# A seven-product scheme for half of a feed-forward matrix, interleaved with tiles of the other matrix

## What is computed

```
f = rms_norm(h, g_ffn_pre)                       # 256 x 2048
f = square(relu(f @ w_ff1)) @ w_ff2              # w_ff1: 2048 x 8192, w_ff2: 8192 x 2048
h = h + rms_norm(f, g_ffn_post)
```

## Time and profile before

| | us |
|---|---|
| median of 3 runs | 2151.79 |
| lowest, highest | 2151.78, 2152.73 |
| profiled execution, first to last instruction (span) | 2150.6 |

### The profile page before, as it was taken

One profiled execution on the slowest core, in us unless ns is written; L12 is line 12 of the kernel. 1 busy time (PEld: TensorE's weight loads), 2 busy tenths in 40 slices (PEclk: granted clock), 3 DMA queues, 4 the chain that ended last, 5 costly groups with the idle time before them and its releaser, 6 DMA issues. The chain is left out here.

```text
span 2150.6 us, 29240 instructions
## 1 busy us (share of the span) xinstructions
PE 2125.1 (99%) x11602; PEld 1841.8 (86%) x11602; DVE 1361.9 (63%) x1979; ACT 1106.1 (51%) x1541; POOL 156.2 (7%) x78
## 2 busy tenths in 40 slices
PE   8999999999999999999999999999999999999998
PEld 7888888888988888888888888888888888888886
DVE  5554568875577558876578678766555555555555
ACT  4444554454464555555455455656435534544543
POOL 0000000000000000000007873000000000000000
PEclk9999999999999999999999999999999999999999
DMA  8666545655576655655656654646666666666664
GB/s 278 196 189 187 165 138 174 179 172 186 185 214 186 178 148 159 174 167 176 191 180 198 193 178 151 215 136 206 193 193 190 189 193 193 189 194 190 192 190 145
DMA packets 325031, 395.17 MB, mean 184 GB/s; under 512 B 20848, under 2 KB 252912, under 8 KB 324128
## 3 DMA queue, kind: packets, MB, share of 16 engines
q1 hardware_dynamic: 323104, 383.21, 59.0%
q0 software_dynamic: 1792, 10.10, 1.2%
HBM read 391.16 MB, written 2.10 MB: 183 GB/s over the span
## 5 line engine op out<-in xcount | busy, mean ns | idle before, releaser
L490 DVE TENSOR_TENSOR low<-raw,high 128x1024 fp32r<-128x1024 f32 (+2 forms) x672 | 809.9, 1209 | 639.0 <-ACT high L934 635.3
L934 ACT ACTIVATE high<-raw 128x1024 fp32r<-128x1024 f32 (+2 forms) x732 | 763.0, 1046 | 775.8 <-PE acc L682 201.7
L682 PE MATMUL acc<-xhl,high 128*128 128x512 f32 x3198 | 766.4, 391 | 0.0
L682 PEld LDWEIGHTS acc<-xhl,high 128*128 128x128 f32 x3198 | 587.0, 188 | 113.8 <-issue 0.7
L699 PE MATMUL acc<-xhl,low 128*128 128x256 f32 x3200 | 436.9, 286 | 1.9 <-DVE xhl L1792 1.4
L699 PEld LDWEIGHTS acc<-xhl,low 128*128 128x128 f32 x3200 | 414.4, 191 | 18.1 <-DVE xhl L1792 1.8
L686 PE MATMUL acc<-high,yhl 128*128 128x512 f32 (+1 forms) x1036 | 380.1, 373 | 2.2 <-DVE work L1718 1.6
L687 PE MATMUL acc<-high,yhl 128*128 128x512 f32 (+1 forms) x1036 | 378.8, 372 | 0.0
L702 PE MATMUL acc<-low,yhl 128*128 128x512 f32 (+1 forms) x1036 | 241.9, 374 | 0.2
L686 PEld LDWEIGHTS acc<-high,yhl 128*128 128x128 f32 x1036 | 195.2, 188 | 36.8 <-DVE work L1718 2.0
L687 PEld LDWEIGHTS acc<-high,yhl 128*128 128x128 f32 x1036 | 195.2, 188 | 33.8
(11 more groups left out here) (228 smaller groups left out, 1286.9 us busy)
## 6 DMA issues: line engine op xcount, KB each, us to landing
raw<-in_w_in SPq DMA_DIRECT2D x328, 512.0 KB, 3.7
raw<-in_w_ff SPq DMA_DIRECT2D x256, 512.0 KB, 3.9
raw<-in_w_out SPq DMA_DIRECT2D x91, 512.0 KB, 4.3
raw<-in_w_mem_kv SPq DMA_DIRECT2D x32, 512.0 KB, 5.0
raw<-in_w_in SPq DMA_DIRECT2D x16, 256.0 KB, 2.7
raw<-in_w_out SPq DMA_DIRECT2D x10, 256.0 KB, 2.8
x_nat<-in_mem SPq DMA_DIRECT2D x4, 512.0 KB, 7.8
x_nat<-in_x POOLq DMA_DIRECT2D x4, 512.0 KB, 6.4
```

Source lines behind the costliest of these rows:

```text
L490: eng.tensor_tensor(part(low, g), part(raw, g), part(high, g).bitcast(F32), ALU.subtract).then_inc(ready, 1)
L682: ins = pe.matmul(acc[:, 2 * (c.acc % 2) + s, :], wh[:, t, at], vhl, start=first, stop=last)
L934: act.activation(part(high, g), part(raw, g), ACT.Copy).then_inc(high_ready, 1)
```

## The change

The second matrix is cut into two column halves. In columns 0 to 1023, of the first 7168 hidden features, each group of 256 features is multiplied as a 2x2 by 2x2 product of blocks (128x128 by 128x512) by Strassen's scheme with seven products in place of eight; there are 28 such groups, four to a run. Their seven sums of the weight blocks are made by VectorE (`group_sums`), split by ScalarE (`split_h`) and VectorE (`split_l`), and the matching sums of the hidden features by GpSimd (`pair_sums`, four additions of 128x128 per pair of tiles). The seven products of a run stay in seven PSUM banks; after the run VectorE adds them to sums in SBUF (`sums_out`), and at the end mixes these into the result (`mix_sums`). Columns 1024 to 2047, and the last 1024 features of all columns, are plain "pieces" of one block each.

The first matrix, after its first 512 columns, comes in tiles of 128 columns and two blocks each (rows of 512 bytes in HBM), all accumulated in one PSUM bank (`feature_tile`), which ScalarE copies out (`tile_copy`) before the next tile. Between them stand the groups, cut in a high and a low half. The order is written out by hand in `ff_order`, and matching orders in the queues. The low part of a block is now written over the block itself, so its load waits until TensorE has used the block four back. The squares of x stand in ScalarE's queue ahead of the first period. The clearing of the sums in SBUF moves from VectorE to GpSimd.

The diff, cut to what the text speaks of (in the order of the file; `ff_period` and `piece_run` appear twice, first ScalarE's, then VectorE's):

```diff
-            add(("f2", q, n), a["w_ff2_2"][0], col, width=width, row0=D * q)
+    w = a["w_ff1_2"][0]
+    run(*[chunk(("f1", 0, j), w, 256 * j, width=256, flipped=True) for j in range(2)])
+    w2 = a["w_ff2_2"][0]
+    for kind, *at in FF_ORDER:
+        if kind == "tile":
+            add(("g1", at[0]), w, P * at[0], width=P, nk=8)
+        elif kind == "piece":
+            e, n, i = at
+            if i == 0:
+                chunk(("f2", e, n), w2, CW * n, row0=8 * P * e, kts=8)
+            place(by["f2", e, n], i)
...
+FF0 = BLOCK2 + BLOCK2_SLOTS
+TILES, TILES_AHEAD = 64, 4
+GROUPS, RUNS = 28, 7
+BESIDE = {0: (6, 7), 1: (None, 8), 2: (9, 10), 3: (None, 11)} | {j: (2 * j + 4, 2 * j + 5) for j in range(4, GROUPS)}
+def ff_order():
+    yield from (("tile", 4), ("tile", 5))
+    for j in range(GROUPS):
+        yield ("high", j)
+        if BESIDE[j][0] is not None:
+            yield ("tile", BESIDE[j][0])
+        yield ("low", j)
+        yield ("tile", BESIDE[j][1])
+        if j % 4 == 3:
+            yield from (("piece", j // 4, n, i) for n in (2, 3) for i in range(4))
+    for i in range(2):
+        for n in range(2):
+            yield ("piece", RUNS, n, i)
+            yield ("tile", 60 + 2 * i + n)
+    yield from (("piece", RUNS, n, i) for i in (2, 3) for n in range(2))
+    yield from (("piece", RUNS, n, i) for n in (2, 3) for i in range(4))
+FF_ORDER = list(ff_order())
+FF1 = FF0 + 8
+BLOCKS = FF1 + sum({"tile": 2, "piece": 1}.get(k[0], 0) for k in FF_ORDER)
+PRODUCTS = ((5, 1, 4), (6, 4, 5), (2, 2, 2), (3, 3, 7), (7, 5, 6), (4, 6, 3), (1, 0, 0))
+OUTS = (2, 3, 1, 5, 6, 7, 4)
...
         def low_part(eng, g, ready):
             eng.wait_ge(high_ready, g + 1)
-            eng.tensor_tensor(part(low, g), part(raw, g), part(high, g).bitcast(F32), ALU.subtract).then_inc(ready, 1)
+            out = part(rawr if g >= FF1 else low, g)
+            eng.tensor_tensor(out, part(raw, g), part(high, g).bitcast(F32), ALU.subtract).then_inc(ready, 1)
...
+            def feature_tile(n):
+                if n > TILES_AHEAD + 1:
+                    pe.wait_ge(tile_out, n - TILES_AHEAD)
+                    if n - 12 in range(0, 56, 8):
+                        pe.wait_ge(piece_out, 4 * ((n - 12) // 8) + 3)
+                bank = tile_bank(n)
+                for i, g in enumerate(by["g1", n].blocks):
+                    wh, wl = part(high, g), part(rawr, g)
...
+                    if i:
+                        with_low()
+                        ins = with_high()
+                    else:
+                        with_high()
+                        ins = with_low()
+                    ins.then_inc(block_used, 1)
...
+            def group_high(j):
+                pe.wait_ge(pair_ready, j + 1)
+                pe.wait_ge(split_high, 3 * j + 3)
+                for p, unit, n in PRODUCTS:
+                    if j % 4 == 0:
+                        product_released(j // 4, p)
+                    for hl in range(2):
+                        pe.matmul(bank_of[p], rows_of(hl, j, n), bset_r[:, j % 2, 7 + unit, :], start=j % 4 == 0 and hl == 0,
+                                  stop=False)
+            def group_low(j):
+                pe.wait_ge(split_low, 3 * j + 3)
+                for p, unit, n in PRODUCTS:
+                    ins = pe.matmul(bank_of[p], rows_of(0, j, n), bset_r[:, j % 2, unit, :], start=False, stop=j % 4 == 3)
+                ins.then_inc(group_used, 1)
...
+            def piece(e, n, i, rows=(0, 1)):
+                g, pair = by["f2", e, n].blocks[i], 4 * e + i
+                wh, wl = part(high, g), part(rawr, g)
+                banks = last_banks[n]
+                pe.wait_ge(pair_ready, pair + 1)
...
+            def x_squares(c):
+                act.wait_ge(norm_ready, norms(2, 2 * c + 1))
+                squares(x[:, :, CW * c:CW * c + CW], c, junk=ff_junk)
...
+            def tile_copy(n):
+                act.wait_ge(block_used, last_of(("g1", n)))
+                if n >= TILES_AHEAD + 2:
+                    act.wait_ge(pair_sq, n // 2)
+                act.activation(tcopy[:, n % 2, :], tile_bank(n), ACT.Copy).then_inc(tile_out, 1)
...
+            def ff_period(j):
+                n, b = next_blocks(j), BESIDE[j][0] is not None
+                p = {0: 2, 1: 3, 2: None, 3: 4}[j] if j < 4 else j + 1 if j % 4 else None
+                if j == 3:
+                    relu_of(p)
+                if j < 4 or j % 4:
+                    tile_copy(BESIDE[j - 1][1] if j else 5)
+                if b:
+                    round_block(n[2])
+                if j + 1 < GROUPS:
+                    split_h(j + 1, 0)
+                if p is not None and j != 3:
+                    relu_of(p)
+                if b:
+                    round_block(n[3])
+                if j + 1 < GROUPS:
+                    split_h(j + 1, 1)
+                    split_h(j + 1, 2)
+                if b:
+                    tile_copy(BESIDE[j][0])
+                if p is not None:
+                    pair_h(p)
+                m = n[4:6] if b else n[2:4]
+                round_block(m[0])
+                round_block(m[1])
+                return m[1] + 1
...
+            cross_out(("f1", 0, 0))
+            round_block(FF1 + 2)
+            relu_of(0)
+            round_block(FF1 + 3)
+            cross_out(("f1", 0, 1))
+            split_h(0, 0)
+            pair_h(0)
+            split_h(0, 1)
+            split_h(0, 2)
+            round_block(FF1 + 4)
+            tile_copy(4)
+            relu_of(1)
+            round_block(FF1 + 5)
+            pair_h(1)
+            for c in range(4):
+                x_squares(c)
+            for j in range(GROUPS):
+                g = ff_period(j)
+                if j % 4 == 3:
+                    piece_run(j // 4, g)
+            g = BLOCKS - 24
+            for b, task in enumerate((None, None, None, None, None, 60, None, None, 61, 30, None, None, 62, None, None, 63)):
+                if b >= 2:
+                    round_block(g + b)
+                if task in (60, 61, 62, 63):
+                    tile_copy(task)
+                if task == 63:
+                    relu_of(31)
+                    pair_h(31)
+                if b == 9:
+                    relu_of(30)
+                if b == 10:
+                    pair_h(30)
+            for b in range(16, 24):
+                round_block(g + b)
+                if b in (18, 19):
+                    act.wait_ge(sum_ready, sums("f2", b - 18))
+                    squares(m_cols(b - 18), b - 18, junk=tail[:, 2, :])
+            act.wait_ge(sum_ready, sums("f2", 2))
+            squares(m_cols(2), 2, junk=tail[:, 2, :])
             for s in range(ST):
-                act.wait_ge(sum_ready, sums("f2", NQ - 1, NF - 1) + s)
-                squares(mixed_cols(FCOLS[NF - 1]), NF - 1, (s,))
-                act.wait_ge(var_ready, 7 + s)
+                act.wait_ge(sum_ready, sums("f2", 3) + s)
+                squares(m_cols(3), 3, (s,), junk=tail[:, 2, :])
+                act.wait_ge(var_ready, 6 + s)
                 act.activation(std[:, s:s + 1], var[:, s:s + 1], ACT.Sqrt).then_inc(std_ready, 1)
...
+            def group_sums(g):
+                units = bset[:, g % 2]
+                dve.wait_ge(group_landed[g % 2][0], 16 * (g // 2 + 1))
+                dve.tensor_tensor(units[:, 1, :], units[:, 1, :], units[:, 0, :], ALU.subtract).then_inc(sum_step, 1)
+                dve.wait_ge(group_landed[g % 2][1], 16 * (g // 2 + 1))
+                dve.wait_ge(sum_step, 3 * g + 1)
+                dve.tensor_tensor(units[:, 4, :], units[:, 3, :], units[:, 1, :], ALU.subtract).then_inc(sum_step, 1)
+                dve.wait_ge(sum_step, 3 * g + 2)
+                t2 = units[:, 4, :].unsqueeze(1).broadcast_to([P, 2, CW])
+                dve.tensor_tensor(units[:, 5:7, :], t2, units[:, 0:3:2, :], ALU.subtract).then_inc(sum_step, 1)
...
+            def ff_period(j):
+                n, b = next_blocks(j), BESIDE[j][0] is not None
+                p = {0: 2, 1: 3, 2: None, 3: 4}[j] if j < 4 else j + 1 if j % 4 else None
+                if j == 3:
+                    fold_pair(p)
+                if j + 1 < GROUPS:
+                    group_sums(j + 1)
+                if p is not None and j != 3:
+                    fold_pair(p)
+                if b:
+                    low_block(n[2])
+                if b:
+                    low_block(n[3])
+                if j + 1 < GROUPS:
+                    for part_no in range(3):
+                        split_l(j + 1, part_no)
+                if j % 4 == 3:
+                    sums_out(j // 4, OUTS[:3])
+                if p is not None:
+                    pair_l(p)
+                m = n[4:6] if b else n[2:4]
+                low_block(m[0])
+                low_block(m[1])
+                return m[1] + 1
...
+            def piece_run(e, g):
+                p = 4 * e + 5
+                sums_out(e, OUTS[3:5])
```

(83 more changed lines are left out.)

367 lines of the change are left out of this document (260 added, 107 removed).

## The result

The changed kernel takes **2204.95 us** (median of 4 runs, 2204.15 to 2207.38) against 2152.26 for the kernel before (4 runs, 2151.78 to 2153.29): ratio **1.0245**, 95% interval 1.023 to 1.0259. The forecast was slower, but 2165 with a range to 2182; it missed by 40 us and lies outside its range.

A forecast was written before the change was run, and what follows sets the result against it. TensorE alone was taken to set the time of the feed-forward part. -19.1 + 3.6 + 3.5 + 2.3 + 9.4 + 1.5 + 11.4 = +12.6, say +13, on a span of 2150.6 gave 2165 us, range 2150 to 2182.

The forecast's parts named there:

- -19.1: Second matrix's groups: 28 groups with three matmuls less each at 0.228 us, -19.1 us, all on the path.
- TensorE's gaps at the seams: Start and end of feed-forward: TensorE waits 2.3 before first group, 9.4 before tile 6, then 2.7, 3.9 and 4.8 us.
- Additions: GpSimd's four 128x128 additions per pair: 0.5 us each, holding VectorE back by about that, 8 us a run.
- rival 3: The port: GpSimd's additions and VectorE's operations alternate, delaying ReLU and rounds in each run's pieces; 2182 us, chance 0.12.
- DMA: Steady state: tile blocks in 512-byte rows, 2.5 us per block, 13.3 of 15.9 us a period; fits, costs nothing.
- rival 4: Short rows bind: a 512-byte packet costs as much as 1 KB, a period needs 17.4 of 15.9; 2207 us, chance 0.04.
- VectorE's load: Steady state: VectorE has 66.5 of 85.2 us a run, 74.5 with the additions' hold-up; fits on average.
- 0.6 us a run, 3.6 for six: Fourth piece of each run: its low part is done at 24.5 against a start at 24.0; bounds 0 and 2.
- Run 0's term, +3.5: Run 0's two short periods of 10.3 us: low parts late by 1.0, 0.2 and 2.2; +3.5 us, bounds 0 and 5.
- +1.5: Start seam: half-rate clock behind the long gap before tile 6, +1.5 us, bounds 0 and 3.
- Second tiles: Tile copies within a period: ScalarE's work, some 11 of 15.9 us, was said to fit; no wait was priced.
- The end seam, 11.4: Last 24 blocks: +2.7 for tile 62's copy, +3.9 after tile 63, +4.8 at the last block; bounds 7 and 14.

The follow-up runs named there:

- run 2: Not a follow-up kernel: the third stretch of four groups and their pieces inside one execution, counted from 0; in the changed kernel its third piece's block took 6.09 us to land.
- the mended kernel: Changed kernel with VectorE's and ScalarE's steps reordered in pieces, periods, start and end, squares moved, and last four blocks loaded early: 2148.46 us, ratio 0.9979.
- later group loads: Changed kernel with each group's 1 MB load issued one step later on the sync queue: 2312.12 us, ratio 1.0736.
- the pair-sum edit: Changed kernel with VectorE's pair sum ahead of the four product sums at the head of each piece stretch: 2182.87 us, ratio 1.0138.
- the period order: Changed kernel with pair sum, ReLU, square and first split ahead of each period's last roundings: 2203.08 us; on top of the pair-sum edit 2172.46 us.

## Why the prediction was right or wrong

**Right.** *-19.1*: 84 matmuls less, as said. *TensorE's gaps at the seams*: before the first group 3.3 (2.3 forecast), before tile 6 7.9 (9.4), before tile 63 2.7 (2.7), pair 31 5.1 (3.9), last block 2.2 (2.0). *Memset*: 1.38, 1.81 and 1.82 us, 5.0 together, as estimated. *Additions*, in part: the groups of GpSimd show

```profile
L2392 POOL TENSOR_TENSOR combo<-combo 128x128 f32<-128x128 f32 x28 | 34.8, 1242 | 2.2
L2387 POOL TENSOR_TENSOR combo<-combo 128x128 f32<-128x128 f32 x28 | 14.8, 528 | 523.5 <-ACT combo L1479 523.5
```

so 0.53 on average (forecast 0.5), but 1.24 for the fourth. With no two-input instruction of VectorE beside it an addition took 0.46; the fourth took 1.32 where it began during one, in 25 of 28 pairs, and VectorE's 1024-column subtraction then took 1.47 instead of 1.22 (in run 2 two of them 2.86 together). That a GpSimd operation and a two-input one of VectorE hold each other up is the exclusive lock that the Trainium skill describes ("SBUF — State Buffer", Who interferes with whom); the trace agrees in kind. In price the forecast was too high: it took 8 us a run off VectorE, but VectorE is busy only 13.3 us less in all seven runs without the additions (1526.1 to 1512.8), 1.9 a run. In time they are worth 5.5 us of the mended kernel, not the 17 that rival 3 added. *DMA*: over 1500 to 2100 us the DMA view gives

```profile
DMA packets 128545, 109.99 MB, mean 183 GB/s; under 512 B 3344, under 2 KB 107792, under 8 KB 128510
...
q1 hardware_dynamic: 128510, 109.52, 61.1%
```

61.1% of 16 engines over 600 us is 5866 us for 109.52 MB, 18.7 bytes per ns; before it was 1024 bytes in 55 ns, 18.6. Rows of 512 bytes cost nothing extra, and rival 4 falls. The Trainium skill ("DMA: Bandwidth & Descriptors", Specifications) puts the least size for full rate at 512 bytes, and the trace agrees. *VectorE's load*: 138 of 180 us in 1640 to 1820 is 77%, just under the 78 to 87% that 66.5 and 74.5 of 85.2 are. No engine was full.

**Wrong.** The forecast added up to +12.6, the trace to +53.1, 40.5 more. Of these 9.8 are run waits (13.4 for 3.6), 24.8 clock and ends of matmuls (26.3 for 1.5) and 8.5 second tiles (for nothing); run 0 (2.8 for 3.5), the start (11.2 for 11.7) and the end's waits (10.0 for 11.4) came out 2.6 lower together.

1. *"0.6 us a run, 3.6 for six"*: the step that failed. Runs 1 to 6 waited 13.4 us at the fourth piece. The chain was right, one term in it was not: "a low part whose data came late (19.3)". In run 2 the high part starts at 1706.7, so the forecast wanted that low part done at 1726.0; it was done near 1728.5. The 19.3 comes out with the 3.9 us median landing of the earlier trace rows, but a group's 1 MB is issued just ahead of the block on the same queue, and it took 6.09. I had added up the bytes of a period (13.3 of 15.9, fits) and never asked for the landing of the one block on the chain. All behind it moved by 2.5 us, and the last low part ran beside GpSimd's additions and took some 0.3 longer: forecast 24.5, measured 27.4 after the high part. Run 6 has no group's load in front and no additions; the chain of waits of the changed kernel, then that of the kernel with later group loads in run 2, show its block:

```profile
2084.74 4.02 DMA raw<-in_w_ff
...
1764.82 3.69 DMA raw<-in_w_ff
```

The landing of the third piece's block and the wait at the fourth piece, us:

| run | changed kernel | later group loads |
|---|---|---|
| 1 | 5.50, 2.63 | 3.80, 0.96 |
| 2 | 6.09, 3.22 | 3.69, 0.55 |
| 3 | 5.34, 2.46 | 3.68, 0.83 |
| 4 | 4.86, 2.07 | 4.29, 1.10 |
| 5 | 4.73, 2.10 | 3.67, 0.74 |
| 6 | 4.02, 0.92 | 3.92, 0.81 |

In all twelve the wait is the landing less 2.6 to 3.2 us. With a landing of about 3.9 the forecast's 0.6 is nearly met, with the group in front it is missed by 1.5 to 2.6. But the late landing costs only in this order of VectorE's queue; the pair-sum edit takes the waits off and leaves the landings as they were.

Run 0's term, +3.5, came out as 2.8 in two waits, of 0.6 and 2.2 us, where its block landed in 3.8. The pair-sum edit took these off too, so they were also a matter of that order and not only of the two short periods.

2. *Clock: "+1.5"*: the largest miss in size. I priced one slow stretch, behind the long gap of the start. The trace has slow stretches behind waits of 2.1 to 3.2 us too, in four of seven runs and over the end, about 19 us by the distances between starts: 5 at the start, 6.5 behind the waits of four runs, 6 over the end, and 1.7 at 1432 us, ahead of the change. What such a stretch costs does not follow the length of its wait. In the pair-sum run 12.6 of busy excess went with 9.7 of idle excess; the period order behind it took off 9.8 of idle excess with only 0.7 of busy excess, because the waits that it closed were short, all but one under 1.3 us.

3. *Second tiles: not in the sum*. 8.5 us in eleven waits. I put both tile copies under "fits on average" and did not follow the order in a period, where the copy stands behind two roundings, ReLU, square and splits. The period-order run shows it: they are gone there.

4. *The end seam, 11.4*: TensorE waited 2.7, 5.1 and 2.2, in all 10.0 where 8.6 was forecast; the 2.8 us behind the last block did not come (from the last matmul's start to the end it is 9.7 us, before it was 9.1). The slow clock of 0.82 to 0.88 over 2140 to 2200 us came on top, and mending the end gave back 13.4.

Range and chances rested on the run wait's bounds, "0 and 2", which were taken without a second landing time. Rival 4 came nearest in time (2207), by luck: its mechanism, short rows, is what the DMA rows rule out. Rival 3 (2182) named waits in every run, but for the wrong reason.

**Open.** The 26.3 us of busy excess are split into clock and modelled ends by a count of distances in one execution only. Whether 512-byte loads land later than 1 KB ones beside a group was not tried, nor a second queue for the group loads.

## What to carry to other kernels

When engines are loaded to three quarters on average, price a change by the one latest chain of each period, with the landing time of that block behind whatever is queued in front of it, not by the median. Mend the latest wait first: the period order was worth about 2 us before it and 10 behind it. Price the clock by the stretch and not by the length of the wait: here waits under 1.6 us cost only themselves, and most of those over 2 us brought 1.6 to 2.8 us more. And a load whose buffer is free must not stand on a queue behind one whose buffer isn't: here that cost 107 us.

## What was not expected of the hardware

Waits of 2.1 to 3.2 us, not only long ones, were followed by matmuls at the 1.2 GHz level, six of eight in the changed kernel, while none of the eleven short ones (0.35 to 1.56 us) was: behind the 2.66 us before tile 63 of the changed kernel, eight took 3.60 us instead of 2.0. With the squares moved the wait before tile 6 was 2.88 us and the eight behind it took 2.11, so not every such wait is followed by it; what decides is not settled here. A 128x128 addition of GpSimd took 0.46 us, and 1.32 when it began while VectorE worked on two SBUF inputs. A 512 KB load took 4.2 us in the median, and the first one issued behind a group's 1 MB took 6.05 in the median of 26 (4.7 to 7.6).
